# Idle products in the norms' waits, projections in six banks, x loaded ahead of the weights, and overlapped last token blocks

## The reference, cut to what matters

```python
for i in range(DEPTH):
    h = layer_norm(DN_ALPHA * h + 0.5 * swiglu(h, ffn_w1[i, 0], ffn_w3[i, 0], ffn_w2[i, 0]), ln_g[i, 0], ln_b[i, 0])
    ...
    h = layer_norm(DN_ALPHA * h + mix, ln_g[i, 1], ln_b[i, 1])
    h = layer_norm(DN_ALPHA * h + 0.5 * swiglu(h, ffn_w1[i, 1], ffn_w3[i, 1], ffn_w2[i, 1]), ln_g[i, 2], ln_b[i, 2])
    h = h + (p[i] @ ple_w_proj[i]) * jax.nn.sigmoid(h @ ple_w_gate[i])
```

```python
x = x + hier_moe(rms_norm(x, norm_ffn_g[l]), ...)
return rms_norm(x, norm_final_g)
```

## Time and profile before

| what | value |
|---|---|
| median of 3 runs | 3413.91 us (3410.81 to 3418.68) |
| the profiled execution's own time | 3412.98 us |
| its span, first to last instruction | 3411.2 us |
| TensorE matmul records | 3152.6 us busy, 92% of the span |
| VectorE, ScalarE, POOL | 41%, 14%, 9% of the span |
| mean granted TensorE clock | 0.954 of full speed |
| DMA | 363.17 MB, mean 106 GB/s |

### The profile page before, as it was taken

How to read it: one execution, slowest core, us unless ns; L and a number is a source line. 1 busy time by engine, 2 the same in 40 slices (tenths; PEclk the granted TensorE clock), 3 DMA queues, 4 the chain that set the end, 5 groups by cost and what they waited for, 6 DMA issues and landing times.

```text
span 3411.2 us, 31620 instructions
## 1 busy us (share of the span) xinstructions
PE 3152.6 (92%) x12814; PEld 2171.8 (64%) x12814; DVE 1392.2 (41%) x3036; ACT 471.3 (14%) x1020; POOL 297.2 (9%) x285
## 2 busy tenths in 40 slices
PE   8999999889999999999996899999999999977774
PEld 7886446738888758888644488887465654452221
DVE  6563212426554426553478265534303750021112
ACT  1101010011001110010122110011102540010001
POOL 0000100110000100001113200010002630010000
PEclk9999998799999999999998999999998999979997
DMA  5222212012222242222110122222131001228996
GB/s 192 75 87 80 93 74 74 13 62 81 87 87 94 79 161 100 90 90 91 75 52 25 62 81 87 87 99 75 60 150 50 1 13 74 74 106 339 384 393 263
DMA packets 56838, 363.17 MB, mean 106 GB/s; under 512 B 6000, under 2 KB 6128, under 8 KB 18160
## 3 DMA queue, kind: packets, MB, share of 16 engines
q1 hardware_dynamic: 45504, 322.98, 25.3%
q10 hardware_dynamic: 8880, 29.73, 2.2%
q0 software_dynamic: 2304, 8.39, 0.7%
HBM read 335.91 MB, written 25.17 MB: 106 GB/s over the span
## 4 chain that ended last, share of the span: by engine, by line
PE 83%; DMA 7%; DVE 6%; POOL 2%; issue 1%; ACT 1%; SPq 1%; ACTq 0%; POOLq 0%; DVEq 0%
PE bank L774 43%; PE bank L466 24%; DMA ring<-in_weights 6%; PE bank L475 4%; PE bank L2399 2%; PE bank L1411 2%; PE bank L502 2%; PE bank L496 1%; POOL area L1751 1%; PE bank L1633 1%; PE bank L1655 1%; PE bank L1438 1%; DVE stat L1700 1%; DMA buf_a<-in_x 1%; DVE area L1945 1%
## 5 line engine op out<-in xcount | busy, mean ns | idle before, releaser
L466 PE MATMUL bank<-area,ring 128*128 128x512 f32 (+1 forms) x1220 | 452.5, 531 | 33.1 <-DVE area L1541 15.7
L466 PEld LDWEIGHTS bank<-area,ring 128*128 128x128 f32 x1220 | 213.8, 193 | 267.1 <-issue 231.2
L774 PE MATMUL bank<-buf_a,mixed 128*128 128x256 f32 x1408 | 319.8, 379 | 0.0
L774 PE MATMUL bank<-buf_b,mixed 128*128 128x256 f32 x1408 | 319.2, 379 | 0.0
L774 PEld LDWEIGHTS bank<-buf_a,mixed 128*128 128x128 f32 x1408 | 268.1, 190 | 36.6
L774 PEld LDWEIGHTS bank<-buf_b,mixed 128*128 128x128 f32 x1408 | 267.5, 190 | 36.4
L466 PE MATMUL bank<-buf_b,ring 128*128 128x512 f32 x656 | 286.3, 595 | 0.0
L796 DVE TENSOR_TENSOR mixed<-ring 128x512 f32<-128x512 f32 (+1 forms) x124 | 84.1, 678 | 466.5 <-PE bank L774 459.9
L774 PE MATMUL bank<-buf_a,ring 128*128 128x256 f32 x1056 | 248.8, 386 | 16.3 <-DMA buf_a<-in_x 14.5
L774 PE MATMUL bank<-buf_b,ring 128*128 128x256 f32 x1056 | 245.0, 382 | 1.8 <-ACT buf_b L665 1.8
L774 PE MATMUL bank<-area,mixed 128*128 128x256 f32 x1056 | 233.8, 379 | 0.0
(11 more groups left out here) (343 smaller groups left out, 3248.9 us busy)
## 6 DMA issues: line engine op xcount, KB each, us to landing
ring<-in_weights SPq DMA_DIRECT2D x300, 1024.0 KB, 4.8
slots_in<-area ACTq DMA_DIRECT2D x1, 8192.0 KB, 23.5
area<-slots_in SPq DMA_DIRECT2D x16, 512.0 KB, 14.0
slots_out<-area ACTq DMA_DIRECT2D x16, 512.0 KB, 8.5
buf_a<-in_x ACTq DMA_DIRECT2D x4, 512.0 KB, 17.9
turn_tables<-area ACTq DMA_DIRECT2D x4, 512.0 KB, 2.7
area<-turn_tables ACTq DMA_DIRECT2D x4, 512.0 KB, 4.6
out<-area ACTq DMA_DIRECT2D x4, 512.0 KB, 2.7
```

The costliest lines, as they stand in the source:

```text
L466: mm = pe.e.matmul(bank[0:w.shape[1], 0:n], w, x[k], start=k == 0, stop=k == len(pieces) - 1)
L774: mm = pe.e.matmul(b, w[:, k * P:(k + 1) * P], x(INPUT_OF[p], unit.lo + k), start=(unit.key, BANK_OF[p]) not in begun, stop=unit.last and ...
```

## The change

1. `idle_products(n)`: n products of 128 columns, whose result nobody reads, into the bank that held the squares, after VectorE has read it. Six stand after the spread of the means and six after the spread of the scale in the layer norms `ffn0`, `ab`, `ffn2`, `c`; six after the fold of the squares and three after the spread of the scale in the RMS norms `ple1`, `nsa`. None in `ffn1` and `ffn3`.
2. In `ffn1` and `ffn3` the scale takes the named bank b3, and the projections go round six banks: b4, b5, b6, b7, b0, b1, b4, b5. The first four gate products then take b6, b7, b0, b1. The order of the products on TensorE and of the copies on ScalarE is as before.
3. SyncE loads block 0, waits for `x_loaded[1]`, loads block 1, waits for `x_loaded[3]`, then loads the others. `N_LEAD[0]` becomes 1.
4. The last token blocks: eight buffers for eight gathers with no wait between them; the squares of a block have a buffer of two and a sum of their own per block; VectorE adds block b before it finishes block b - 1, and ScalarE's queue is ordered to suit. Six semaphores are merged into three elsewhere, with the same waits.

```diff
     def plan_mean(st, beside=None):
         i = NORMS.index(st)
+        order = [(g.turn + j) % 8 for j in range(8)]
         g.add(("mean", st), (mean_read, i + 1))
...
+        g.add(("means", st), (means_read, i + 1))
+        if beside is None:
+            plan_scales(st)
+            return
+        others = itertools.cycle(order[4:] + order[:2])
+        for m in range(KD):
+            if m == KD // 2:
+                plan_scales(st, order[3])
+            beside(m, next(others))
+        g.turn = next(others)
...
+    def idle_products(pe, label, read, n):
+        pe.wait_ge(*read)
+        for _ in range(n):
+            pe.e.matmul(bank(label)[:, 0:P], C("ident"), C("mean"), start=True, stop=True)
...
         spread(pe, ("means", st), mean_c)
+        if st not in BESIDE:
+            idle_products(pe, ("squares", st), (square_read, STATS[st] + 1), IDLE_ROOT)
...
         spread(pe, ("scales", st), scale_c)
+        if st not in BESIDE:
+            idle_products(pe, ("squares", st), (square_read, STATS[st] + 1), IDLE_RMS if st in RMS else IDLE_SCALE)
...
-    N_LEAD = {0: 2, 1: 4, 2: 4, 3: 4}
+    N_LEAD = {0: 1, 1: 4, 2: 4, 3: 4}
...
         for b in range(TB):
-            scalar_final(ac, b, (summed, 2 * b + 2))
+            scalar_final_sum(ac, b, (summed, 2 * b + 2))
+            if b:
+                scalar_final_store(ac, b - 1)
+            scalar_final_root(ac, b)
+        scalar_final_store(ac, TB - 1)
...
-            vector_final(ve, b)
+            if b:
+                vector_final(ve, b - 1)
+        vector_final(ve, TB - 1)
...
         for n in range(2 * TB):
-            if n > 3:
-                po.wait_ge(summed, n - 3)
-            po.e.indirect_dma_start(out=ys[n % 4], ...
+            po.e.indirect_dma_start(out=ys[n], ...
...
-        load_blocks(sy, g, 0, common_blocks)
+        load_blocks(sy, g, 0, 1)
+        sy.wait_ge(x_loaded[1], 16)
+        load_blocks(sy, g, 1, 2)
+        sy.wait_ge(x_loaded[KD // 2 - 1], 16)
+        load_blocks(sy, g, 2, common_blocks)
```

More of the change, by code:

```diff
@@ L2 @@
+import itertools
 from contextlib import ExitStack
@@ L510, in bank @@
         return banks[(groups or g).bank[label]]
+    BESIDE, IDLE_ROOT, IDLE_SCALE, IDLE_RMS = ("ffn1", "ffn3"), 6, 6, 3
     sums, square_sums = norm[:, 0:T], norm[:, T:2 * T]
@@ L552, in plan_mean, with plan_squares, plan_scales @@
         i = NORMS.index(st)
+        order = [(g.turn + j) % 8 for j in range(8)]
         g.add(("mean", st), (mean_read, i + 1))
-        plan_squares(st, True, beside)
-    def plan_squares(st, mean=False, beside=None):
         g.add(("squares", st), (square_read, STATS[st] + 1))
[L558 to L562, removed]
+        g.add(("means", st), (means_read, i + 1))
[8 more added lines that the diff above has]
+        g.turn = next(others)
+    def plan_squares(st):
+        g.add(("squares", st), (square_read, STATS[st] + 1))
+        plan_scales(st)
+    def plan_scales(st, bank=None):
+        g.add(("scales", st), scale_used(st), bank=bank)
     def scale_used(st):
@@ L1063, in scalar_load_p, with plan_ple_proj @@
         ac.e.dma_start(pt, io["p"][layer].rearrange("(c p) t -> p c t", p=P)).then_inc(p_loaded, 16)
-    def plan_ple_proj(layer, ms):
-        for m in ms:
-            g.add(("proj", layer, m), (proj_done, KD * layer + m + 1), blocks=B(f"ple{layer}_proj", m))
+    def plan_ple_proj(layer, m, bank):
+        g.add(("proj", layer, m), (proj_done, KD * layer + m + 1), blocks=B(f"ple{layer}_proj", m), bank=bank)
     def tensor_ple_proj(pe, stream, layer, ms):
@@ L2318, in build_in, with scalar_final_sum, scalar_final_root, scalar_final_store @@
     final_sum, final_mean, final_sqrt, normed = sem("final_sum"), sem("final_mean"), sem("final_sqrt"), sem("normed")
-    final_square, final_s = region(12288, D), stat[:, 92:93]
-    def scalar_final(ac, b, ready):
+    final_square, final_s = [region(12288, D), region(18432, D)], [stat[:, 92 + b:93 + b] for b in range(TB)]
+    def scalar_final_sum(ac, b, ready):
         ac.wait_ge(*ready)
-        if b:
-            ac.wait_ge(normed, b)
-        ac.e.activation(final_square, xt[b], ACT.Square, accum_out=final_s).then_inc(final_sum, 1)
+        if b > 1:
+            ac.wait_ge(final_sum, b - 1)
+        ac.e.activation(final_square[b % 2], xt[b], ACT.Square, accum_out=final_s[b]).then_inc(final_sum, 1)
+    def scalar_final_root(ac, b):
         ac.wait_ge(final_mean, b + 1)
-        ac.e.activation(final_s, final_s, ACT.Sqrt).then_inc(final_sqrt, 1)
+        ac.e.activation(final_s[b], final_s[b], ACT.Sqrt).then_inc(final_sqrt, 1)
+    def scalar_final_store(ac, b):
         ac.wait_ge(normed, b + 1)
@@ L2343, in build_in @@
     turned_back = sem("turned_back")
-    landed = [sem(f"landed{i}") for i in range(4)]
+    landed = [sem(f"landed{i}") for i in range(2 * TB)]
     EP = NEXP // 2
@@ L2348, in build_in @@
     e_hidden, e_turned = [region(20480 + i * 256, 256) for i in range(2)], [region(20992 + i * 256, 256) for i in range(2)]
-    ys = [region(2048 + i * D, D) for i in range(4)]
+    ys = [region(2048 + i * D, D) for i in range(6)] + rows_in[1:3]
     def expert_weights(p, e, k):
@@ L2608, in build_in @@
     plan_ffn(1)
-    plan_mean("ffn1", lambda: plan_ple_proj(0, range(0, 4)))
-    plan_ple_proj(0, range(4, KD))
+    plan_mean("ffn1", lambda m, b: plan_ple_proj(0, m, b))
     plan_ple(0)
@@ L2616, in build_in @@
     plan_ffn(3)
-    plan_mean("ffn3", lambda: plan_ple_proj(1, range(0, 4)))
-    plan_ple_proj(1, range(4, KD))
+    plan_mean("ffn3", lambda m, b: plan_ple_proj(1, m, b))
     plan_ple(1)
```

48 lines of the change are left out of this document (25 added, 23 removed).

## The result

| | before | after |
|---|---|---|
| median of the runs | 3416.3 us (3410.81 to 3425.33) | 3377.14 us (3370.22 to 3390.61) |
| ratio, 95% interval | | 0.9888 [0.9847, 0.9928] |
| the profiled execution, its span | 3412.98, 3411.2 us | 3372.44, 3370.6 us |
| mean granted TensorE clock | 0.954 | 0.964 |

A forecast was written before the change was run, and what follows sets the result against it. TensorE, busy 92% of the span, was taken as the bound, through its granted clock and waits. Terms 8 + 11.7 + 1.5 + 4.5 + 2.5 + 5.6 = 33.8 us off 3412.98 gave 3379.2, stated as 3380; range 3368 to 3395.

The forecast's parts named there:

- start: Kernel start: weights held back let x land earlier, part four near 13.5 us, unit 1 ending at 35.5; 8 us.
- `ffn0`, `ffn2`: Two layer norms: idle products keep the clock up in and behind them; 3.3 and 2.4 us.
- `ab`, `c`: Two layer norms: idle products shrink two pauses and keep the clock up; 2.4 and 3.6 us.
- `ple1`, `nsa`: RMS norms: idle products bring the clock back earlier, in `nsa` some 4 us into the router's records; 1.5 and 4.5 us.
- projections, `ffn1` and `ffn3`: Six banks start the gate products 3.6 and 4.2 us earlier, less 2.65 each at half clock; 2.5 us together.
- last token blocks: Kernel end: blocks follow every 4.45 us instead of 5.71, gathers in time; 5.6 us.
- attention of the second block: No gain forecast; clock phase at some twenty other places was to move the time by 2 or 3 us.
- rival three: At the start, x is slow by its own small packets, so the start gives nothing: 3388 us, chance 0.06.
- Idle products: In layer norms: at full clock both groups fit the waits and cost nothing, 0.23 us a product; 11.7 us won together.
- rival two: In the norms, idle products don't hold the clock, too few columns passing; 17.7 us not won: 3402 us, chance 0.11.
- Experts: Expert stage, from about 3085 us: weights set the pace, nothing touches it, and whatever is won earlier is kept.
- The upper bounds written beside the terms: Highest gain allowed per term, such as 10.5 us for the start; all together were said to reach 3371 us.

The follow-up runs named there:

- Run 3: Changed kernel with all six weight blocks issued at once, one leading unit kept: 3387.9 us (one execution).
- run 7: Changed kernel with twice the idle products in each wait of a norm (12, 12 and 6): 3389.36 us.
- Run 1: Changed kernel without any idle products, all else as changed: 3396.37 us.
- run 2: Changed kernel with idle products of 32 columns instead of 128, same number: 3401.46 us (one execution).
- Runs 5: Changed kernel with ScalarE's copies of projections 4 to 7 inside `ffn1` and `ffn3`, and six products in the mixes' pause of `ab` and `c`: 3364.32 us.
- 9: Changed kernel with ScalarE's copies inside `ffn1` and `ffn3`, the mixes' pause filled, and the second block's attention pauses filled: 3360.6 us.
- 11: Changed kernel with only six products added in the mixes' pause of `ab` and `c`: 3373.05 us (one execution).
- run 10: The changed kernel run and profiled again with no edit: 3379.06 us.
- Run 4: Changed kernel with ScalarE's copies of projections 4 to 7 moved inside the norms `ffn1` and `ffn3`: 3368.92 us.
- Run 8: Changed kernel with the fifth to eighth gathers waiting for sums again: 3392.67 us (one execution).
- runs 6: Changed kernel with four products in each 1.02 us pause of the second block's attention: 3373.84 us.

## Why the prediction was right, and where not

The time, 3377.14, is 2.9 us under the forecast and inside the range. The terms against the profiled spans (from the starts of the steps named above and their mates of before; rounded):

| term | predicted | measured |
|---|---|---|
| start | 8 | 10.8 |
| `ffn0`, `ffn2` | 3.3, 2.4 | 3.0, 2.4 |
| `ab`, `c` | 2.4, 3.6 | 1.5, 2.5 |
| `ple1`, `nsa` | 1.5, 4.5 | 1.5, 5.2 |
| projections, `ffn1` and `ffn3` | 0.95, 1.6 | 1.3, 1.3 |
| last token blocks | 5.6 | 4.9 |
| attention of the second block | 0 | 5.8 |
| the rest, net | 0 | 0.4 |
| sum | 33.8 | 40.6 |

**Start: right mechanism, too small.** The prediction put part four of x at 13.5 us, delayed by block 1, and added 1.7 us behind it for a start at half clock. Unit 1 ended at 33.32 us instead of 35.5. The four transfers of x landed 6.6 to 9.1 us after their issue (9.3 to 21.5 before), so from 7.46 on TensorE did not wait for x again and reached part four at 12.84. The slow records lay ahead of part four and not behind it: the 94 behind it took 20.5 us where the prediction had 20.3 and 1.7. That is 1.5 of the 2.8 us missing; 0.7 is part four, and 0.6 is what the prediction rounded off 8.6. The 10.8 us are near the top of what this start gives: the slow records last up to 13 us in other profiles, and over the eleven of them the gain lies between 9.6 and 10.9. Run 3 shows that holding the weights back is the cause, which settles rival three.

**Idle products: right.** "At full clock both groups fit and cost nothing" holds to 0.01 us a product (0.223 against 0.23; run 7). Run 1 puts their worth at 17.4 us by stretches and 19 by medians against the 17.7 forecast (against the kernel before, the same six norms gained 16.1), and that rejects rival two for 128 columns; run 2 suggests that with 32 columns it would have come true in part.

**`ab` and `c`: the one step that was wrong.** "With the products the two pauses shrink from 1.64 and 1.70 us to some 0.4 each" is true, but there are three pauses. The prediction looked at those on both sides of the scale's spread and not at the one ahead of the first spread, which is 0.18 us in `ffn0` but 1.65 in `ab` and `c`, as VectorE has four mixes to do there before it copies the mean. The clock fell in it or just behind it and cost the spread 0.9 us in `ab`, and in `c` mostly the six products behind the spread (2.77 us instead of 1.50). So 0.9 of the 2.4 us in `ab` and 1.1 of the 3.6 in `c` were missing. Runs 5, 9 and 11 fill the pause and lose nothing. By run 10 it is only a chance of loss: there `ab` gave its 2.4 us in full.

**RMS norms: right.** The router's records began at 0.11 us and fell to half clock 5 us in (2993.5), as estimated: narrow records did not hold the clock. That loss is still there. `nsa` gave 5.2 us for 4.5, 4.9 of them in the router's records.

**Projections: right.** "The new first wait is for banks b0 and b1": the gate products wait 5.23 us on a copy of ScalarE (L1102), then lose 2.1 and 2.7 us at half clock, where 2.65 each was taken. Run 4 takes the wait away and gets the rest, 7.3 and 7.9 us; the upper bound of 7.8 for both together was of another kind, as it left the copies where they are. No run takes the six banks back alone; the row of the new wait and run 4 carry this.

**Last blocks: the order does it.** The interval of 4.45 us came as worked out (4.46). The 0.7 missing lie in the waits of the third and fourth sum for their gathers, 0.18 and 0.67 us: the prediction followed only the eighth gather. Run 8 leaves the four added buffers worth a few tenths at most.

**Attention: not foreseen.** "The phase of the clock at some twenty other places moves the time by 2 or 3 us" is the sentence that failed in size. This one stretch was 481.8 to 499.2 us in the eleven profiles in which its pauses are open, and 479.7 and 482.1 in the two in which they are filled (runs 6 and 9). Against the 487.6 of before, the two profiles of the changed kernel stand 5.8 us better and 8.4 worse. So the 5.8 of the 40.6 us cannot be put down to the change, and the sum without them, 34.8, is nearer the forecast. The medians' 39 us hold the same lottery, with an interval of some 14 us either way. What decides it within an execution is not settled beyond what run 10 shows.

**Experts: kept, but by luck to 0.4 us.** "Whatever is won earlier is kept" holds for the two profiles compared here (350.8 and 350.4 us from the router's records to the first sum). Over all thirteen this stage took 343.9 to 357.8 us, and the prediction gave it no spread at all.

**How much of the agreement is luck.** The terms on which the change acts give 34.4 us by the profiles against 33.8. That rests in part on errors that cancel: the start and `nsa` gave 3.5 us more, `ab`, `c` and the last blocks 2.7 less. With stages that move by 14 and 17 us from one execution to the next, a median within 2.9 us of the forecast is better than this method can promise. The upper bounds written beside the terms also add up to 47.5 us, a time near 3366, and not to the 3371 that the prediction states.

## What to carry to other kernels

Fill the waits of a saturated TensorE with products that end before the wait does, and list every pause of the place first, not only the widest ones; price them from a record of the trace first: six products in a wait of 1.7 us ended before it did, and twelve made the six norms 8.2 us longer. A periodic pause of 1 us inside dense work can cost the clock even where one profile shows it at full there; filled, the stretch took 479.7 and 482.1 us where it had been anywhere up to 499.2, though the medians do not yet show that gain clear of noise. Where the profile of one execution decides between versions, compare stretches, and profile the same kernel twice before reading anything into one that has no edit.

## What the runs showed of the hardware

- The same kernel with the same pauses (1.02 us once a round) ran a stretch of attention at full clock in one execution and in alternate 10 us at half clock in another, 14 us apart.
- A matmul record of 32 columns with a full 128 x 128 f32 weight took as long as one of 128 columns (1.42 and 1.50 us for twelve), and held the clock in two of the six norms where the wide ones were put.
- The pause of 1.65 us for the mixes, the only one over 0.45 us left in its norm, cost the clock in 7 of 12 places with six products in the other waits; where it was filled too, and none over 0.45 us was left, in none of 6.
- With one weight block beside x its four transfers landed 6.6 to 9.1 us after their issue, and TensorE never waited for x after 7.46 us; with six blocks beside it they took 9.2 to 21.4 us, and TensorE waited 3.2 us each for parts two and three, the last time until 22.36.
- At the very start TensorE's records took twice their later time (2.04 us for four at 7.46, 1.03 at 12.84), while the granted clock of that stretch reads 1.00.
